# Residuals and squares made piece by piece at the borders, modulation tiles set into attention waits, eight gate units set into the second attention

## The chip, the cores and the metric

One core of one Trainium2 chip runs the whole program. The metric is the device time of one execution in microseconds (us), median of several runs.

## What is computed

Two transformer blocks over 256 tokens of width 2048, all in f32. The parts that matter here, cut from the reference:

```python
def first_block(...):
    for layer in range(2):
        mod = silu(c) @ ada_w[layer] + ada_b[layer]
        shift, scale, gate = split(mod)
        h = rmsnorm(x, norm_g[layer]) * (1 + scale) + shift
        ...                     # layer 0: attention of 8 heads and convolution; layer 1: spatial gating
        x = x + gate * (mixed @ w_out)
    return rmsnorm(x, final_g)

def second_block(x, c, ...):
    sh1, sc1, g1, sh2, sc2, g2 = split(silu(c) @ w_ada + b_ada)
    h = rms_norm(x, norm1_w) * (1 + sc1) + sh1
    q, k, v, f_logit, u, gate_s, gate_a = split(h @ w_in)
    y_ssm = half_glu(s5_mixer(u, ...), w_glu, b_glu)
    y_attn = fox_attention(q, k, v, f_logit, ...)          # 8 heads, causal, forget gates
    merged = sigmoid(gate_s) * (y_ssm @ w_ssm_up) + sigmoid(gate_a) * (y_attn @ w_attn_up)
    x = x + g1 * (merged @ w_out)
    h2 = rms_norm(x, norm2_w) * (1 + sc2) + sh2
    return x + g2 * peer_ffn(h2, ...)                      # 128 experts per token, gathered by row
```

## The kernel before

Everything lies with features in partitions: x, h and proj hold tiles of 128 features by 256 tokens (TOK), 16 tiles for a width of 2048 (DT). A matrix product is a row of **units**. A unit is one output tile: 16 matmuls of 128x128 weights by 128x256 into a bank of PSUM (G0 or G1, in turn), done by `dense` and `unit` (L417). ScalarE takes each unit out of its bank (`leave`, L860), with the gate's factor where it feeds a residual (`leave_gated`). Weights come in chunks of 1 MB, one per unit, through a ring of four slots: SyncE issues a load as soon as the units of the chunk four back are done. The order of the stages is the list STREAM (L60), and the host packs the weights in that order; each engine's program is written out by hand in the same order, and engines meet at semaphores.

The stages in order: `first`, `ev`, `kv`, `ez`, `zb` (projections of layer 0, with the first attention among them), `ev_out`, `od`, `od_out` (layer 1), `w_in`, `glu`, `ssm_up`, the second attention, `attn_up`, `gates` (32 units), `w_out`, `peer_q`, then the experts.

**Modulation tiles.** Each output of `silu(c) @ ada_w` is a dot product of a row of 2048 on VectorE (`ada_tile`, L1238), a tile of 1 MB at a time, 16 tiles to a group. Tiles come through a second ring of four (`aring`), whose loads GpSimd issues when VectorE has used the tile four back (L382). Group g must be done before its shift, scale or gate is used. `ada_part(g, first, count)` places tiles in VectorE's program.

**Borders.** Between two blocks x gets its residual, the squares of x are summed over features, and the root of the mean scales x. `add_residual` (L1543) waits for each four tiles of h, adds them to x (L1548), squares them (L1539) and adds the four squares up (L1215); TensorE sums over partitions with a matrix of ones into B7 (`feature_sum_of_fours`, L468); ScalarE takes the root (`std`, L882), VectorE the reciprocal (L1223) and writes x/rms into h by fours (L1556); ScalarE applies scale and shift (`modulate`, L892), after which the next dense stage can start on tile 0. At `ev_out` VectorE's program has modulation groups 1 and 2 whole ahead of `add_residual`, at `od_out` group 6. After `od_out` there are two normalizations in a row: the last of the first block, with weight final_g, made in x (L1604), and the first of the second block, on squares of its result.

**Attention.** Per head: TensorE makes scores, VectorE maxima, ScalarE exponentials, VectorE probabilities, TensorE turns them (L531), ScalarE copies them (L920), TensorE multiplies with the values (L538), VectorE takes the result (`finish`). `softmax`, `softmax_steps` and `attention` take a table `between` of what each engine does after head hh. In the first attention that is a `zb` unit on TensorE and two or three modulation tiles on VectorE; in the second, after heads 0, 2, 4 and 6, one chunk of `ssm_up`, which is four output tiles of 4 matmuls each.

**Gates.** After `attn_up` 32 gate units follow: 16 of gate_s into proj 0 to 15 and 16 of gate_a. VectorE multiplies them with the up results and adds the halves; `merged` lets `w_out` start. Modulation groups 7 and 8 stand ahead of this, group 9 between the first 16 products and the rest.

## Time and profile before

| | us |
|---|---|
| median of 3 runs | 3271.11 (3262.88 to 3278.96) |
| profiled execution, its own time | 3271.55 |
| its span, first to last instruction | 3269.7 |
| TensorE busy (matmul) | 2762.1, 84% |
| VectorE busy | 2081.1, 64% |
| GpSimd busy | 840.3, 26% |
| ScalarE busy | 579.1, 18% |
| mean granted clock of TensorE | 0.899 of full |

Busy time on TensorE is a poor measure of what it achieves, since its clock has two levels, 1.2 and 2.4 GHz (0.5 and 1.0 of full in the views). What bounds the end is read from the chain of waits; where TensorE stops or runs slowly is read from the timeline and from the granted clock of short windows.

### The profile page before, as it was taken

How to read it: one execution, taken by the hardware profiler on the slowest of the kernel's cores; microseconds unless marked ns; L12 is line 12 of the kernel's file. 1: busy time of each engine (PE TensorE's matmuls, PEld its weight loads, DVE VectorE, ACT ScalarE, POOL GpSimd, SP SyncE). 2: the span in 40 equal slices, each digit the busy share in tenths (PEclk: the TensorE clock that was granted, in tenths of full speed). 3: DMA queues.
4: the chain of work that ended last, by engine and by line, in shares of the span. 5: the costliest groups of instructions: out<-in, count | busy, mean ns of one | idle time of the engine just before them, and what ended most of it. 6: DMA issues, size and time to landing. Idle time of an engine off the chain costs nothing.

```text
span 3269.7 us, 31515 instructions
## 1 busy us (share of the span) xinstructions
PE 2762.1 (84%) x12106; PEld 2206.7 (67%) x12106; DVE 2081.1 (64%) x2892; ACT 579.1 (18%) x1102; POOL 840.3 (26%) x724
## 2 busy tenths in 40 slices
...
GB/s 375 383 390 134 112 195 396 301 188 355 305 355 280 157 107 113 122 44 140 421 262 268 143 140 408 374 382 418 421 421 387 380 337 206 385 399 390 378 397 267
DMA packets 158373, 951.27 MB, mean 291 GB/s; under 512 B 17584, under 2 KB 17584, under 8 KB 69808
## 3 DMA queue, kind: packets, MB, share of 16 engines
...
## 4 chain that ended last, share of the span: by engine, by line
PE 41%; DVE 23%; DMA 23%; ACT 6%; issue 4%; POOL 2%; DVEq 0%; ACTq 0%; POOLq 0%
PE G L417 33%; DMA acc<-v_rows,proj 12%; DMA aring<-ada 7%; DVE vec L1830 3%; DVE aring L1238 3%; DVE aring L1802 2%; ACT vec L1116 2%; PE M L810 2%; DVE ring L1802 2%; DVE proj L1319 2%; DVE proj L1489 1%; DMA aring<-peer_u,proj 1%; PE G L798 1%; DMA ring<-peer_u,proj 1%; DVE proj L1843 1%
## 5 line engine op out<-in xcount | busy, mean ns | idle before, releaser
L417 PE MATMUL G<-h,ring 128*128 128x256 f32 x4928 | 1084.6, 383 | 13.2 <-ACT h L892 13.2
L417 PEld LDWEIGHTS G<-h,ring 128*128 128x128 f32 x4928 | 944.8, 192 | 147.4 <-issue 16.5
L382 POOL DMA_DIRECT2D aring<-ada x208 | 109.8, 529 | 1631.3 <-DVE mods L1238 1624.3
L1238 DVE CUSTOM_DVE_ANT_0 aring<-aring,acc,vec 128x2048 f32<-128x2048 f32 x176 | 410.9, 2350 | 174.8 <-DMA aring<-ada 173.5
L417 PE MATMUL G<-proj,ring 128*128 128x256 f32 x2080 | 462.0, 386 | 10.6 <-DVE proj L1595 4.8
L1830 DVE SCALAR_TENSOR_TENSOR vec<-acc,dots,vec 128x1024 f32<-128x1024 f32 x254 | 325.9, 1283 | 203.7 <-DMA acc<-v_rows,proj 201.4
L417 PEld LDWEIGHTS G<-proj,ring 128*128 128x128 f32 x2080 | 402.9, 194 | 69.9 <-issue 12.8
L849 PE MATMUL M<-sq,mix 128*128 128x512 f32 x1024 | 442.5, 595 | 1.8 <-ACT mix L1130 1.1
L849 PEld LDWEIGHTS M<-sq,mix 128*128 128x128 f32 x1024 | 195.3, 191 | 248.4 <-issue 245.5
L405 POOL DMA_INDIRECT acc<-v_rows,proj x256 | 274.1, 1071 | 316.1 <-DVE vec L1830 293.3
L397 POOL DMA_INDIRECT aring<-peer_u,proj x128 | 219.7, 1716 | 347.3 <-DVE proj L1768 222.8
L1802 DVE CUSTOM_DVE_ANT_0 aring<-sq,aring 128x2048 f32<-128x2048 f32 x108 | 245.4, 2290 | 29.5 <-DMA aring<-peer_u,proj 19.1
L860 ACT ACTIVATE proj<-G 128x256 f32 (+1 forms) x170 | 65.3, 384 | 980.6 <-PE G L417 980.4
L397 POOL DMA_INDIRECT ring<-peer_u,proj x112 | 209.1, 1867 | 102.1 <-PE M L810 31.3
L1802 DVE CUSTOM_DVE_ANT_0 ring<-sq,ring 128x2048 f32<-128x2048 f32 x91 | 207.1, 2290 | 17.4 <-DMA ring<-peer_u,proj 16.3
L820 PE MATMUL B<-h,acc 128*128 128x128 f32 x704 | 97.4, 305 | 51.9 <-ACT acc L1140 29.0
L1140 ACT ACTIVATE acc<-M 128x1024 f32<-128x1024 f32 x86 | 86.9, 1024 | 269.1 <-PE M L810 268.9
L798 PE MATMUL G<-vec 128*128 128x128 f32 x256 | 59.1, 405 | 88.1 <-ACT vec L1124 85.7
L820 PEld LDWEIGHTS B<-h,acc 128*128 128x128 f32 x704 | 95.3, 221 | 54.8 <-issue 30.4
L798 PEld LDWEIGHTS G<-vec 128*128 128x128 f32 x256 | 49.9, 290 | 95.2 <-ACT vec L1124 92.7
L810 PE MATMUL M<-cst,ring 128*128 128x128 f32 x336 | 63.2, 368 | 56.8 <-DMA ring<-peer_u,proj 56.8
L1548 DVE TENSOR_TENSOR x<-x,h 128x1024 f32<-128x1024 f32 x12 | 14.7, 1225 | 151.3 <-ACT h L860 151.2
...
## 6 DMA issues: line engine op xcount, KB each, us to landing
...
sq<-v_blocks SPq DMA_DIRECT2D x128, 512.0 KB
...
acc<-v_rows,proj POOLq DMA_INDIRECT x256, 6.8
...
```

Source lines behind the costliest of these rows:

```text
L382: pool.dma_start(aring[:, n % SLOTS, :], ada[a]).then_inc(ada_in[n % SLOTS], 16)
L397: pool.indirect_dma_start(u_slot(n), None, peer_u, where).then_inc(u_in[ROW_SLOT[n]], 16)
L405: pool.indirect_dma_start(v_ring[:, n % VSLOTS, :], None, v_rows, where).then_inc(v_in[n % VSLOTS], 16)
L417: mm = nc.tensor.matmul(bank[:, 0:TOK], lhsT=ring[:, slot, weights_at + t * P:weights_at + (t + 1) * P], rhs=rhs[:, t, :], start=(t == 0), ...
L798: mm = nc.tensor.matmul(G[n % 2][:, k * P:(k + 1) * P], lhsT=far[:, k * P:(k + 1) * P], rhs=near[:, k * P:(k + 1) * P], start=True, stop=True)
L810: mm = nc.tensor.transpose(M[:, j * P:(j + 1) * P], u_slot(n)[:, j * P:(j + 1) * P], ident)
L820: mm = nc.tensor.matmul(O[k % 2][:, 0:P], lhsT=turned_row[:, j * P:(j + 1) * P], rhs=tokens, start=(j == 0), stop=(j == DT - 1))
L849: mm = nc.tensor.matmul(M[:, tk * HALF + half * 512:tk * HALF + (half + 1) * 512], lhsT=mix[tk][:, j, :], rhs=blocks[:, j % BSLOTS, half * ...
L1140: nc.scalar.activation(turned_row[:, half * 1024:(half + 1) * 1024], M[:, half * 1024:(half + 1) * 1024], ACT.Copy).then_inc(row_kept, 1)
L1238: V_.tensor_tensor_reduce(out=tile, in0=tile, in1=vector, scale=1.0, scalar=bias, op0=ALU.mult, op1=ALU.add, accum_out=column).then_inc(ad ...
L1802: V_.tensor_tensor_reduce(out=u_slot(n), in0=sq[:, tk * D:(tk + 1) * D], in1=u_slot(n), scale=1.0, scalar=0.0, op0=ALU.mult, op1=ALU.add, ...
L1830: V_.scalar_tensor_tensor(out=y, in0=v_ring[:, n % VSLOTS, :], scalar=c, in1=y, op0=ALU.mult, op1=ALU.add).then_inc(v_added, 1)
```

## The change

1. `PIECES` cuts the 16 tiles into 4, 4, 4, 3 and 1. `add_residual(name, k)` does one piece, and the pieces stand among the modulation tiles of `ev_out` and `od_out`; at `w_out` they follow each other. The pieces of 3 and 1 are not added up on VectorE; TensorE sums each of their tiles. x/rms goes into h as 1, 3, 4, 4, 4.
2. Between the two blocks only one pass of squares is left. gs2 is final_g squared; TensorE sums squares as they are (B7) and weighted with gs2 (B6), piece by piece among the units of `od_out`. var2 is the product of the weighted sum and 1/rms squared, h is x times the product of both reciprocals, and final_g goes into the scale gs. The values of x itself are normalized after the second attention.
3. The tiles of group 0 and five of group 1 are spread over the waits ahead of and in the first attention (a new table `waiting`, ahead of the wait for the values product).
4. Eight units of gate_a (tiles 4 to 7 and 12 to 15) leave the gates stage: fill0 ahead of glu, fill1 (three) ahead of the second attention, fill2 to fill5 after heads 1, 3, 5 and 7. `gates` has 24 units. ScalarE makes their sigmoid in two operations at `attn_up`.
5. Group 9 of the modulation tiles is cut in two halves, before and behind unit 20 of the gates.

```diff
+PIECES = ((0, 4), (4, 4), (8, 4), (12, 3), (15, 1))
...
-          ("glu", 1, 4), ("ssm_up", 4, 4), ("attn_up", 8, 2), ("gates", 32, 1), ("w_out", 16, 1), ("peer_q", 16, 1)]
+          ("fill0", 1, 1),
+          ("glu", 1, 4), ("fill1", 3, 1), ("up0", 1, 4), ("fill2", 1, 1), ("up1", 1, 4), ("fill3", 1, 1), ("up2", 1, 4),
+          ("fill4", 1, 1), ("up3", 1, 4), ("fill5", 1, 1), ("attn_up", 8, 2), ("gates", 24, 1), ("w_out", 16, 1), ("peer_q", 16, 1)]
...
+            def sum_piece(t, n, added):
+
+                sums[0] += 1
+                pe.wait_ge(sum_in, sums[0])
+                if n == 4:
+                    at = t * TOK if added is sq else t * P
+                    return nc.tensor.matmul(B7[:, 0:TOK], lhsT=ones, rhs=added[:, at:at + TOK], start=(t == 0), stop=False)
+                for e in range(t, t + n):
+                    mm = nc.tensor.matmul(B7[:, 0:TOK], lhsT=ones, rhs=sq[:, e * TOK:(e + 1) * TOK], start=False,
+                                          stop=(e == DT - 1))
+                return mm
+
+            def residual_sum():
+
+                for t, n in PIECES:
+                    mm = sum_piece(t, n, sq)
                 mm.then_inc(sum_done, 1)
+
+            def residual_sums(k):
+
+                t, n = PIECES[k]
+                mm = sum_piece(t, n, att)
+                if k == len(PIECES) - 1:
+                    mm.then_inc(sum_done, 1)
+                for e in range(t, t + n):
+                    mm = nc.tensor.matmul(B6[:, 0:TOK], lhsT=gs2[:, e:e + 1].to_broadcast([P, P]), rhs=sq[:, e * TOK:(e + 1) * TOK],
+                                          start=(e == 0), stop=(e == DT - 1))
+                if k == len(PIECES) - 1:
+                    mm.then_inc(both_sums, 1)
 
...
-            dense("od_out", [proj])
-
-
-            feature_sum_of_fours()
-            feature_sum(sq, DT, 4)
+            dense("od_out", [proj], first=0, count=6)
+            residual_sums(0)
+            dense("od_out", [proj], first=6, count=4)
+            residual_sums(1)
+            dense("od_out", [proj], first=10, count=4)
+            residual_sums(2)
+            dense("od_out", [proj], first=14, count=2)
+            residual_sums(3)
+            residual_sums(4)
...
+            dense("fill0", [h])
...
             pe.wait_ge(ssm_g, 4)
             dense("glu", [proj, proj, proj, proj], k=4)
+            dense("fill1", [h], count=1)
             pe.wait_ge(head_used, 1)
             head_rows_spread(8, row=1)
...
+            dense("fill1", [h], first=1, count=1)
...
+            dense("fill1", [h], first=2, count=1)
...
-                      {0: lambda: ssm_up(0), 2: lambda: ssm_up(1), 4: lambda: ssm_up(2), 6: lambda: ssm_up(3)})
+                      {0: lambda: ssm_up(0), 1: lambda: dense("fill2", [h]), 2: lambda: ssm_up(1), 3: lambda: dense("fill3", [h]),
+                       4: lambda: ssm_up(2), 5: lambda: dense("fill4", [h]), 6: lambda: ssm_up(3), 7: lambda: dense("fill5", [h])})
             pe.wait_ge(o_read, 16)
             dense("attn_up", [proj[:, 12:20, :], proj[:, 12:20, :]], k=8)
-            dense("gates", [h], count=16)
-            dense("gates", [h], first=16, count=16)
+            dense("gates", [h])
...
+                    if hh in waiting:
+                        waiting[hh]()
                     dve.wait_ge(pv_done, base + hh + 1)
...
             head_inverse(1)
+            ada_part(0, 0, 1)
             step(head_scale(sq[:, 0:1024], 4, V("k_norm")), on=rot_in)
+            ada_part(0, 1, 3)
             step(rope(kv_keys[:, :, 0:TOK], 2, 2), on=qk_ready)
+            ada_part(0, 4, 3)
...
-                    {0: lambda: ada_part(0, 0, 3), 1: lambda: ada_part(0, 3, 2), 2: conv_centre,
-                     3: lambda: ada_part(0, 5, 3), 4: lambda: ada_part(0, 8, 2), 5: conv_scale,
-                     6: lambda: ada_part(0, 10, 3), 7: lambda: ada_part(0, 13, 3)})
+                    {0: lambda: ada_part(0, 8, 1), 1: lambda: ada_part(0, 10, 1), 2: conv_centre,
+                     3: lambda: ada_part(0, 13, 1), 4: lambda: ada_part(0, 15, 1), 5: conv_scale,
+                     6: lambda: ada_part(1, 2, 1), 7: lambda: ada_part(1, 4, 1)},
+                    {0: lambda: ada_part(0, 7, 1), 1: lambda: ada_part(0, 9, 1), 2: lambda: ada_part(0, 11, 1),
+                     3: lambda: ada_part(0, 12, 1), 4: lambda: ada_part(0, 14, 1), 5: lambda: ada_part(1, 0, 1),
+                     6: lambda: ada_part(1, 1, 1), 7: lambda: ada_part(1, 3, 1)})
...
+            def add_residual(name, k, added=None):
+
+                t, n = PIECES[k]
+                dve.wait_ge(unit_evac, UNIT0[name] + t + n)
+                xs, squares = flat(x[:, t:t + n, :]), sq[:, t * TOK:(t + n) * TOK]
+                step(tt(xs, xs, flat(h[:, t:t + n, :]), ALU.add))
+                step(tt(squares, xs, xs, ALU.mult), on=None if n == 4 else sum_in)
+                if n == 4:
+                    add_tiles(squares if added is None else added[:, 512 * k:512 * k + 512], squares, 4)
+
+            def scaled_into_h(by):
+
+                for t, n in ((0, 1), (1, 3), (4, 4), (8, 4), (12, 4)):
+                    step(tt(h[:, t:t + n, :], x[:, t:t + n, :], over_tiles(by, n), ALU.mult), on=h_scaled)
 
...
+            ada_part(1, 5, 7)
+            add_residual("ev_out", 0)
+            ada_part(1, 12, 4)
+            ada_part(2, 0, 3)
+            add_residual("ev_out", 1)
+            ada_part(2, 3, 7)
+            add_residual("ev_out", 2)
+            ada_part(2, 10, 6)
+            add_residual("ev_out", 3)
+            add_residual("ev_out", 4)
...
-            ada_group(6)
-            add_residual("od_out")
+            step(tt(gs2[:, :], V("final_g"), V("final_g"), ALU.mult))
+            norm_weight(gs[:, :], V("norm1_w"), mod("scale2"))
+            step(tt(gs[:, :], gs[:, :], V("final_g"), ALU.mult))
+            for k in range(len(PIECES)):
+                if k < 4:
+                    ada_part(6, 4 * k, 4)
+                add_residual("od_out", k, added=att)
             root()
-            for t in range(DT):
-                V_.scalar_tensor_tensor(out=x[:, t, :], in0=x[:, t, :], scalar=V("final_g")[:, t:t + 1], in1=rstd[:, :],
-                                        op0=ALU.mult, op1=ALU.mult).then_inc(x_normed, 1)
-                if t % 4 == 3:
-                    dve.wait_ge(x_normed, t + 1)
-                    square_four(t // 4, add_up=False)
-            normed_into_h(V("norm1_w"), mod("scale2"))
-            mods_from(6)
+            dve.wait_ge(both_sums, 1)
+            step(tt(var2, rstd[:, :], rstd[:, :], ALU.mult))
+            step(tt(var2, var2, B6[:, 0:TOK], ALU.mult), on=var_in)
+            sums["std"] += 1
+            dve.wait_ge(std_ready, sums["std"])
+            step(V_.reciprocal(var2, var2))
+            step(tt(var2, var2, rstd[:, :], ALU.mult))
+            scaled_into_h(var2)
...
+            act.wait_ge(unit_evac, UNIT0["attn_up"])
+            for t in (20, 44):
+                nc.scalar.activation(flat(proj[:, t:t + 4, :]), flat(proj[:, t:t + 4, :]), ACT.Sigmoid).then_inc(filled, 1)
...
+            for t in range(DT):
+                V_.scalar_tensor_tensor(out=x[:, t, :], in0=x[:, t, :], scalar=V("final_g")[:, t:t + 1], in1=rstd[:, :],
+                                        op0=ALU.mult, op1=ALU.mult).then_inc(x_normed, 1)
...
             step(tt(part(8, 8), part(8, 8), part(28, 8), ALU.mult))
-            ada_group(9)
-            dve.wait_ge(unit_evac, gates + 28)
-            step(tt(part(16, 8), part(16, 8), sq[:, 2048:4096], ALU.mult))
+            dve.wait_ge(filled, 2)
+            step(tt(part(20, 4), part(20, 4), sq[:, 3072:4096], ALU.mult))
+            step(tt(part(44, 4), part(44, 4), part(40, 4), ALU.mult))
+            step(tt(part(4, 4), part(4, 4), part(20, 4), ALU.add))
+            step(tt(part(12, 4), part(12, 4), part(44, 4), ALU.add))
+            ada_part(9, 0, 8)
+            dve.wait_ge(unit_evac, gates + 20)
+            step(tt(part(16, 4), part(16, 4), sq[:, 2048:3072], ALU.mult))
+            step(tt(part(0, 4), part(0, 4), part(16, 4), ALU.add))
+            ada_part(9, 8, 8)
+            dve.wait_ge(unit_evac, gates + 24)
             step(tt(part(24, 4), part(24, 4), part(36, 4), ALU.mult))
-            step(tt(part(0, 12), part(0, 12), part(16, 12), ALU.add))
-            dve.wait_ge(unit_evac, gates + 32)
-            step(tt(part(44, 4), part(44, 4), part(40, 4), ALU.mult))
-            step(tt(part(12, 4), part(12, 4), part(44, 4), ALU.add), on=merged)
+            step(tt(part(8, 4), part(8, 4), part(24, 4), ALU.add), on=merged)
```

TensorE at the end of `od_out`, in the changed kernel (G are the units' banks, L423 the dense helper, L475 and L477 the plain sums, L494 the weighted ones):

```order
L423 MATMUL G<-proj,ring 128x256 x96
L475 MATMUL B<-att,cst 128x256
L494 MATMUL B<-sq,gs 128x256 x4
L423 MATMUL G<-proj,ring 128x256 x64
L475 MATMUL B<-att,cst 128x256
L494 MATMUL B<-sq,gs 128x256 x4
L423 MATMUL G<-proj,ring 128x256 x32
L477 MATMUL B<-sq,cst 128x256 x3
L494 MATMUL B<-sq,gs 128x256 x3
L477 MATMUL B<-sq,cst 128x256
L494 MATMUL B<-sq,gs 128x256
L423 MATMUL G<-h,ring 128x256 x64
```

Before, 4 and then 16 plain sums stood between the last unit of `od_out` and the first of `w_in`; now three groups of five stand among the units, and eight matmuls behind them.

TensorE from the head sums to the first scores of the second attention, before (L489 spreads the inverse norms, L710 turns the values, L513 is a head's scores):

```order
L479 MATMUL B<-sq,cst 8x256 x8
L489 MATMUL M<-dots,cst 128x256 x8
L417 MATMUL G<-proj,ring 128x256 x16
L489 MATMUL M<-dots,cst 128x256 x8
L710 MATMUL M<-cst,proj 128x128 x16
L513 MATMUL M<-proj 128x256
```

And now (L516, L744 and L540 are the same steps):

```order
L506 MATMUL B<-sq,cst 8x256 x8
L423 MATMUL G<-h,ring 128x256 x16
L516 MATMUL M<-dots,cst 128x256 x8
L423 MATMUL G<-proj,ring 128x256 x16
L423 MATMUL G<-h,ring 128x256 x16
L516 MATMUL M<-dots,cst 128x256 x8
L423 MATMUL G<-h,ring 128x256 x16
L744 MATMUL M<-cst,proj 128x128 x16
L423 MATMUL G<-h,ring 128x256 x16
L540 MATMUL M<-proj 128x256
```

Four gate units (those that read h) stand among the steps.

VectorE at unit 20 of the gates, in the changed kernel (L1283 is a modulation tile, its second row reads the accumulator):

```order
L1283 ISA aring,mods<-aring,acc,vec 128x2048
L1283 ISA mods 128x1
L1779 TENSOR_TENSOR proj<-proj,sq 128x1024
L1780 TENSOR_TENSOR proj<-proj 128x1024
L1283 ISA aring,mods<-aring,acc,vec 128x2048
L1283 ISA mods 128x1
```

Eight tiles stand ahead of L1779 and eight behind L1780; behind those come the last product and sum (L1783, L1784). Before, all sixteen stood between the products of unit 16 and those of unit 28.

## Rows read from the trace of the kernel before

**Rows 1.** The page, chain that ended last: shares of the span by line.

```profile
PE G L417 33%; DMA acc<-v_rows,proj 12%; DMA aring<-ada 7%; DVE vec L1830 3%; DVE aring L1238 3%; DVE aring L1802 2%; ACT vec L1116 2%; PE M L810 2%; DVE ring L1802 2%; DVE proj L1319 2%; DVE proj L1489 1%; DMA aring<-peer_u,proj 1%; PE G L798 1%; DMA ring<-peer_u,proj 1%; DVE proj L1843 1%
```

**Rows 2.** Timeline of TensorE: start, duration, line, tiles, count, idle before and releaser.

```profile
504.35 110.77 PE L417 MATMUL G<-proj,ring 128*128 128x256 f32 x512 [1.59 <-DVE proj L1533]
...
641.55 127.30 PE L417 MATMUL G<-h,ring 128*128 128x256 f32 x576 [4.40 <-ACT h L892]
...
1147.29 30.33 PE L417 MATMUL G<-h,ring 128*128 128x256 f32 x128 [4.41 <-ACT h L892]
```

**Rows 3.** Timeline of all engines, the border from ev_out to od.

```profile
615.15 0.47 ACT L860 ACTIVATE h<-G,mods 128x256 f32<-128x256 f32 x1 [6.43 <-PE G L417]
...
621.09 1.22 DVE L1548 TENSOR_TENSOR x<-x,h 128x1024 f32<-128x1024 f32 x1
...
635.93 1.22 PE L468 MATMUL B<-sq,cst 128*128 128x256 f32 x2 [2.49 <-DVE sq L1215]
...
637.76 1.75 DVE L1223 RECIPROCAL rstd<-rstd 128x256 f32<-128x256 f32 x1 [1.68 <-ACT rstd L882]
...
640.80 7.97 ACT L892 ACTIVATE h<-h,mods,gs 128x256 f32<-128x256 f32 x16 [3.15 <-DVE h L1556]
```

**Rows 4.** Timeline of VectorE and of TensorE, first attention.

```profile
399.07 0.42 DVE L1511 TENSOR_TENSOR proj<-B,proj 128x256 f32<-128x256 f32 x1 [2.56 <-PE B L538]
...
418.19 1.09 PE L531 MATMUL M<-cst,att 128*128 128x128 f32 x8 [1.21 <-DVE att L1303]
```

**Rows 5.** Timeline of ScalarE, last eviction of od_out.

```profile
1121.08 0.47 ACT L860 ACTIVATE h<-G,mods 128x256 f32<-128x256 f32 x1 [6.43 <-PE G L417]
```

**Rows 6.** Timeline of TensorE, glu to attn_up.

```profile
1404.04 8.86 PE L417 MATMUL G<-proj,ring 128*128 128x256 f32 x32
...
1412.83 5.00 PE L489 MATMUL M<-dots,cst 8*128 8x256 f32 x16
...
1420.33 3.68 PE L710 MATMUL M<-cst,proj 128*128 128x128 f32 x16 [2.51 <-DVE proj L1272]
...
1435.25 1.22 PE L513 MATMUL M<-proj 128*128 128x256 f32 x2 [2.90 <-ACT att L912]
...
1445.22 9.06 PE L417 MATMUL G<-proj,ring 128*128 128x256 f32 x32
...
1457.39 0.66 PE L531 MATMUL M<-cst,att 128*128 128x128 f32 x4
...
1458.73 1.13 PE L538 MATMUL B<-sq,proj 128*128 128x256 f32 x4 [0.69 <-ACT sq L920]
...
1469.30 8.97 PE L417 MATMUL G<-proj,ring 128*128 128x256 f32 x32
...
1529.37 55.52 PE L417 MATMUL G<-proj,ring 128*128 128x256 f32 x256 [0.88 <-DVE proj L1692]
```

**Rows 7.** Windows of TensorE: length, busy (count), granted clock, DMA share, GB/s.

```profile
1466.00:1469.00 3.00, 2.31 (x8) 0.50 0.00 0
1475.00:1478.00 3.00, 3.00 (x16) 1.00 0.00 0
```

**Rows 8.** End of the gates: timelines, group 9's tiles, window of all engines.

```profile
1695.93 2.29 DVE L1704 TENSOR_TENSOR proj<-proj,sq 128x2048 f32<-128x2048 f32 x1 [51.18 <-ACT proj L860]
...
L1238 DVE CUSTOM_DVE_ANT_0 aring<-aring,acc,vec x16: 2346/2351/2352, 1700.6 to 1753.6; 128x2048 f32<-128x2048 f32 x16
...
1720.00:1750.00 30.00, 30.00 (x140) 26.41 (x140) 17.27 (x15) 1.54 (x4) 2.63 (x5) 1.00 1.02 423
...
1807.68 1.22 DVE L1713 TENSOR_TENSOR proj<-proj 128x1024 f32<-128x1024 f32 x1
...
1809.23 110.77 PE L417 MATMUL G<-proj,ring 128*128 128x256 f32 x512 [3.33 <-DVE proj L1713]
```

**Rows 9.** Timeline of TensorE, end of w_out and start of peer_q.

```profile
1919.84 3.73 PE L738 MATMUL M<-cst,mods 128*128 128x128 f32 x32
...
1929.70 15.74 PE L417 MATMUL G<-h,ring 128*128 128x256 f32 x64 [4.40 <-ACT h L892]
```

72 lines of the change are left out of this document (32 added, 40 removed).

## The prediction, made before the change was run

> **What bounds the kernel now.** The chain that ended last comes first [rows 1]: its largest share, 33% of the span, is TensorE in the dense helper (L417), so what delays the next dense stage delays the end. The timeline of TensorE then shows where it stops between stages [rows 2]: `ev_out` ran 504.35 to 615.1, and `od` began only at 641.55. A dense unit (16 matmuls of 128x256) takes 110.77/16 = 6.9 us, one matmul 0.43. The timeline of all engines over that border [rows 3] shows what fills it: VectorE, busy with modulation tiles, makes its first residual at 621.09, when `ev_out` is long over. In the second attention the timeline of TensorE [rows 6] and its granted clock [rows 7] show waits inside the heads and stretches at 1.2 GHz: glu's 16 matmuls took 8.86 us there, and four up units 9.06, where 6.9 is the full price.
>
> **First attention.** Five more modulation tiles leave the stage behind it, and one tile per head goes into VectorE's wait for the values product. That wait is 2.56 us at head 0 and a tile takes 2.35 [rows 4, 8], so it is hidden; if a tile has not landed, its delay shows. Seven tiles ahead of the heads lie in rotation and norm waits and cost nothing. TensorE's own work stays; what it gains is its waits for the probabilities, 1.21 us at head 2 [rows 4] and a like one at head 5: 1.2 x 2 = **-2.4 us** (ends 0 and -4).
>
> **First border, `ev_out` to `od`.** Now four tiles of x are added and squared as they come; only tile 15 is left at the end. From the end of the last unit, E: TensorE adds 7 sums instead of 4, 7 x 0.43 = 3.0, the last of which needs tile 15's square. That square is ready at E + 0.5 (eviction, as the ACTIVATE of [rows 3]) + 2 x 0.46 (a 128x256 operation is 0.42 [rows 4]) + 0.1 = 1.5, so the sums decide: E + 3.2 with the drain of the last. Then sum end to reciprocal 0.6 (635.93 + 1.22 to 637.76), reciprocal 1.8, first tile of h 0.45 instead of a group of 1.22, bias and scale to matmul 0.75 (640.80 to 641.55): E + 6.8 [rows 2, 3]. I add 0.5, since tiles 1 to 3 come as one group. The gap was 641.55 - 615.1 = 26.4, so **-19.1 us**. It needs the tiles of groups 1 and 2 done before unit 15. In seven tiles four lie in the ring, and the others come every (1753.6 - 1700.6 - 4 x 2.3) / 11 = 4.0 us, the step of tiles that wait for the transfer [rows 8]. With a residual group after units 4, 8 and 12 (27.7 us apart), seven tiles take 4 x 2.3 + 3 x 4.0 = 21 us and fit; the last six start 3.7 us after unit 12 and take 17.2, which ends them as unit 15 arrives and 7 us before unit 16. If they are late, the last pieces are what is late next, at most some 5 us. Ends -14 and -21.
>
> **Second border, `od_out` to `w_in`.** One normalization, its square pass and its second root go: the second variance is the sum of squares weighted by final_g squared, times 1/rms squared. From the last eviction T = 1121.08 to `w_in` at 1147.29 it was 26.2 us [rows 2, 5]. Now: TensorE has 6 matmuls for piece 3 and then 1 for piece 4, T + 3.2 with drain; root and reciprocal 0.6 + 1.8; two 128x256 products on VectorE 0.9; root again 0.7; reciprocal 1.8; product 0.45; first tile 0.45; bias to matmul 0.75: T + 10.7, and 0.5 for the group: 11.2, a gain of 15.0. But the weighted sums cost TensorE 5 matmuls for each of the three first pieces in the middle of the stage, on the path: 15 x 0.43 = 6.5. **-8.5 us** (ends -5 and -10). The 16 normalizing operations move behind the second attention, 16 x 0.42 = 6.7 us of VectorE, covered by its 51.18 us wait at 1695.93 [rows 8].
>
> **Second attention.** Eight gate units, 8 x 6.9 = 55.3 us, leave the gates stage and stand in this one. The new stretch from 1404.04, at full clock: fill0 6.9; glu 6.9; a fill 6.9; spread 3.5 (5.00 was at half clock); a fill 6.9, which covers VectorE's 2.35 before the turning; turning 1.9 (3.68 at half); a fill 6.9, which covers ScalarE's copy; scores 3.2 (from the end of the four up units, 1454.2, to 1457.39); wait for the exponentials 2.9; scores 3.2; turn, copy, product 2.5 (1457.39 to 1458.73 + 1.13) [rows 6]. Sum 51.7. A pair of heads is then 2 x (6.9 + 3.2 + 2.5) = 25.2 instead of 1469.30 - 1445.22 = 24.1: in it the fill costs 1.1. Three pairs 75.6; up, turn and product of the last head 9.4; fill5 6.9. Total 143.6, and 4 us that I allow for stretches at 1.2 GHz around the opening wait, the size of the loss seen on glu and the first up units: 147.6, where it was 1529.37 - 1404.04 = 125.3. So +22.3 - 55.3 = **-33.0 us**. The price of the clock is the least known of all: [rows 7] has 0.50 in the low part of a pair and 1.00 at the end of its up units. If every one of the eight fills and four ups began slow (9.06 - 6.91 = 2.2 each) 22 us would come on top of no allowance, 18 against mine; with no slow stretch it is 4 better. Ends -15 and -37. I take the value near full clock because after the change the low part of a head is followed by 6.9 us of dense work, where before two such parts stood together.
> The Trainium skill (TensorE: Matmul & The Clock Gate, Part 1: The HAM clock gate) says that the slow clock is the default and activity releases it. By that alone the stretch would run at full clock, and the allowance of 4 us would go. The trace agrees in kind: 1.00 at 1475, 0.50 at 1466.
>
> **End of the gates.** Here something is taken back. Sixteen tiles of group 9 used to follow unit 16, and ran 1700.6 to 1753.6 + 2.35 = 1755.9: 55.3 us, since they come at the pace of the transfers (1720 to 1750: DMA share 1.02, 423 GB/s) [rows 8]. Then 50 us were left. Now 8 units, not 16, follow. From T0, where VectorE starts on unit 16's product (1695.93): products 4.7, four 128x1024 operations for the gates made early 5.0, so tiles start at T0 + 9.7; 55.3 of tiles, with the 2.5 us for unit 20 between them covered by the transfer; T0 + 65.0; then a product and a sum, 2.5: `merged` at T0 + 67.5, TensorE at + 67.8. The gates end at T0 - 0.5 + 8 x 6.9 = T0 + 54.8. TensorE stands 13.0 us instead of 3.33, and starts at 1.2 GHz, about 1.2 us more (half of the 2 us that the up units lost, for there is no low work ahead): **+10.9 us**. Queued behind the second eight tiles are unit 24's product, and behind that `w_out`. Ends +5 and +15.
> The Trainium skill (DMA: Bandwidth & Descriptors, Issuing engines are not separate DMA queues) says that loads issued from different engines run on the same 16 DMA engines and interleave. By it the wait stays, since modulation tiles and weights share them; if they did not share, sixteen tiles would take 16 x 2.3 = 37 us and the term would be zero.
>
> **Third border, `w_out` to `peer_q`.** TensorE first makes g3 (3.6 us from 1919.84), then 7 sums 3.0, drain and root 0.8, reciprocal 1.8, tile 0.45, 0.75: 10.4, where it was 1929.70 - 1919.84 = 9.9 [rows 9]. **+0.5 us** (0 to 1). What was late there was VectorE; now it is TensorE's sums.
>
> **Sum.** -2.4 - 19.1 - 8.5 - 33.0 + 10.9 + 0.5 = -51.6. The profiled execution took 3271.55 us, which gives 3219.9; the median of the runs is 0.4 lower, so I say **3220 us**. Everything behind `w_out` (the experts) is only shifted.
>
> **Rivals.**
> *The clock falls once in each pair.* The fills do not keep it up: one up unit group at 9.06 (+2.1) and one low part as in [rows 6] at double price (+2.8) per pair, 4 x 4.9 - 4 = +15.6: 3236. For it: the 0.50 that stands in every pair now. Against it: low parts that follow dense work end at 1.00. Chance 0.17.
> *The modulation tiles come in time at the gates.* Then `merged` waits for unit 24 only and the +10.9 goes: 3209. For it: 3.33 us was the whole wait. Against: the transfer share of 1.02. Chance 0.10.
> *Slower: the second attention runs at 1.2 GHz throughout.* TensorE has some 130 us of work in the new stretch; all of it at half clock is +130 less my 4: 3346. It decides from 52 us on, when more than 40% of that work is slow. For it: from the second spread to the first up units the matmuls of [rows 6] went at half pace (3.68 for the turning). Against: the waits that kept it low are the ones filled. Chance 0.02.
> The forecast has 0.65; 0.06 is left to a border whose gain fails in part (the first at its end -14, the second at -5: 3228) or wholly (3247).
>
> **Range and chances.** The range takes in both nearer rivals and their spread with the bounds of the border terms: 3209 less 5 for the better end of the second attention, 3236 plus 7 for the borders' ends: 3204 to 3243. The likeliest case alone is 3210 to 3230. About 0.5% (16 us) can be told from no change: faster 0.94, within it 0.04, slower 0.02.
>
> **What would show it.** The gap before `od` near 7 us and before `w_in` near 11 from the last eviction; 15 matmuls into B6 and B7 inside `od_out`; pairs of 25 us with clock at or above 0.9; about 13 us of wait before `w_out`, ended by VectorE, with the last tiles ended by DMA. Wrong would be: pairs near 30 us; a residual that starts late after unit 16; a `w_out` that starts within 4 us.

## The result, and the profile after

The changed kernel takes **3231.07 us** (median of 4 runs, 3224.2 to 3235.47), the kernel before on the same chip 3273.87 (4 runs): a ratio of 0.9872, 95% interval 0.984 to 0.9904. That is 42.8 us or 1.3% faster. Forecast were 3220 us and a range of 3204 to 3243: right in direction and inside the range, 11 us short of the gain.

Timeline of TensorE in the changed kernel, in the order of the stages. The columns are those of [rows 2]; the dense helper is L423 now. The profile has two records for each matmul of the program: the 16 matmuls of a unit stand as x32, so a pair of records (x2) is one matmul, and the counts below are records.

```profile
503.35 110.77 PE L423 MATMUL G<-proj,ring 128*128 128x256 f32 x512 [1.55 <-DVE proj L1586]
613.96 1.46 PE L475 MATMUL B<-sq,cst 128*128 128x256 f32 x6
615.25 1.89 PE L477 MATMUL B<-sq,cst 128*128 128x256 f32 x8
620.75 0.67 PE L423 MATMUL G<-h,ring 128*128 128x256 f32 x2 [3.60 <-ACT h L927]
...
986.58 43.39 PE L423 MATMUL G<-proj,ring 128*128 128x256 f32 x192 [4.56 <-DVE proj L1653]
...
1115.91 30.12 PE L423 MATMUL G<-h,ring 128*128 128x256 f32 x128 [6.94 <-ACT h L927]
...
1530.86 55.42 PE L423 MATMUL G<-proj,ring 128*128 128x256 f32 x256
...
1764.73 112.83 PE L423 MATMUL G<-proj,ring 128*128 128x256 f32 x512 [12.70 <-DVE proj L1784]
1877.40 3.73 PE L773 MATMUL M<-cst,mods 128*128 128x128 f32 x32
...
1887.76 0.67 PE L423 MATMUL G<-h,ring 128*128 128x256 f32 x2 [3.60 <-ACT h L927]
```

The starts of the stages make a ledger. "Before" is the same difference in the kernel before [rows 2, 6, 8, 9]; the predicted column regroups the terms of the sum.

| stretch of TensorE | before | after | difference | predicted |
|---|---|---|---|---|
| up to `ev_out` | 504.35 | 503.35 | -1.0 | -2.4 |
| `ev_out` to `od` | 137.20 | 117.40 | -19.8 | -19.1 |
| `od` to `od_out` | 367.03 | 365.83 | -1.2 | 0 |
| `od_out` to `w_in` | 138.71 | 129.33 | -9.4 | -8.5 |
| `w_in` to `attn_up` | 382.08 | 414.95 | **+32.9** | **+22.3** |
| `attn_up` to `w_out` | 279.86 | 233.87 | -46.0 | -45.6 |
| `w_out` to `peer_q` | 120.47 | 123.03 | +2.6 | +1.7 |
| start of `peer_q` | 1929.70 | 1887.76 | -41.9 | -51.6 |

The -41.9 up to `peer_q` is close to the 42.8 us between the medians. The two profiled executions differ by 47.3 us; the other 5.4 lie behind `peer_q`, where no work was changed, and are within the scatter of that stretch (below). All the terms but one came within 1.5 us; the second attention cost 10.6 us more than predicted. Its timeline on TensorE: the head sums and fill0, a spread of head rows and glu, the opening, and some rows of the pairs of heads (the shape is weights, then what is streamed; `8*128 8x256` contracts over 8 rows, `128*8 128x256` over 128 rows into 8 columns):

```profile
1365.28 3.62 PE L506 MATMUL B<-sq,cst 128*8 128x256 f32 x16
1368.83 7.17 PE L423 MATMUL G<-h,ring 128*128 128x256 f32 x32
1375.93 3.71 PE L516 MATMUL M<-dots,cst 8*128 8x256 f32 x16
1379.58 8.86 PE L423 MATMUL G<-proj,ring 128*128 128x256 f32 x32
...
1414.59 0.59 PE L540 MATMUL M<-proj 128*128 128x256 f32 x2
1415.11 0.70 PE L544 MATMUL M<-cst,att 8*128 8x256 f32 x2
...
1420.83 1.22 PE L540 MATMUL M<-proj 128*128 128x256 f32 x2 [2.90 <-ACT att L947]
...
1430.80 8.87 PE L423 MATMUL G<-proj,ring 128*128 128x256 f32 x32
1439.50 0.59 PE L540 MATMUL M<-proj 128*128 128x256 f32 x2
...
1442.77 0.66 PE L558 MATMUL M<-cst,att 128*128 128x128 f32 x4
...
1457.57 7.07 PE L423 MATMUL G<-proj,ring 128*128 128x256 f32 x32
...
1469.09 2.07 PE L565 MATMUL B<-sq,proj 128*128 128x256 f32 x4 [0.69 <-ACT sq L955]
1470.95 7.58 PE L423 MATMUL G<-h,ring 128*128 128x256 f32 x32
...
1482.98 2.08 PE L565 MATMUL B<-sq,proj 128*128 128x256 f32 x4 [0.69 <-ACT sq L955]
1484.85 9.14 PE L423 MATMUL G<-proj,ring 128*128 128x256 f32 x32
```

A group of 32 matmuls takes 7.07 us at full clock; here glu took 8.86, and three behind it 8.87, 7.58 and 9.14. The product with the values (L565) takes 1.13 at full clock and 2.07 and 2.08 in the two rows here. Windows of TensorE in the changed kernel (length, busy and count, granted clock, DMA share, GB/s) show the two levels beside each other. The last window is the whole stretch, from the end of the head sums to `attn_up`:

```profile
1424.00:1427.00 3.00, 3.00 (x7) 0.50 0.00 0
1447.00:1450.00 3.00, 3.00 (x15) 1.00 0.00 0
1484.00:1487.00 3.00, 3.00 (x9) 0.50 0.00 0
...
1368.83:1530.86 162.03, 153.63 (x626) 0.89 0.23 78
```

That stretch was 128.98 us in the kernel before, at 0.74, and is 162.03 now, at 0.89. The clock did rise, but not to full.

### The profile page after: what moved, and what is told of

Same layout as the page of the kernel before. It is cut to its first block, busy times and chain, and to the rows that moved or that the text cites. A ratio compares the mean times of both kernels' runs of the same rounds, so it can differ in the third digit from the quotient of the medians.

```text
span 3222.4 us, 31476 instructions
## 1 busy us (share of the span) xinstructions
PE 2747.6 (85%) x12124; PEld 2203.6 (68%) x12124; DVE 2076.1 (64%) x2899; ACT 577.1 (18%) x1101; POOL 841.1 (26%) x724
## 4 chain that ended last, share of the span: by engine, by line
PE 47%; DVE 21%; DMA 19%; ACT 6%; issue 4%; POOL 2%; DVEq 0%; ACTq 0%; POOLq 0%
PE G L423 37%; DMA acc<-v_rows,proj 12%; DMA aring<-ada 5%; DVE vec L1903 3%; DVE aring L1283 2%; ACT vec L1161 2%; PE M L845 2%; DVE ring L1875 2%; DVE proj L1366 2%; DVE aring L1875 1%; DVE proj L1536 1%; PE G L833 1%; DVE proj L1916 1%; ACT vec L1166 1%; DMA ring<-peer_u,proj 1%
## 5 line engine op out<-in xcount | busy, mean ns | idle before, releaser
L423 PE MATMUL G<-h,ring 128*128 128x256 f32 x4928 | 1086.1, 382 | 14.6 <-ACT h L927 14.6
L423 PEld LDWEIGHTS G<-h,ring 128*128 128x128 f32 x4928 | 944.1, 192 | 149.9 <-issue 17.9
L1283 DVE CUSTOM_DVE_ANT_0 aring<-aring,acc,vec 128x2048 f32<-128x2048 f32 x176 | 410.1, 2350 | 133.4 <-DMA aring<-ada 131.3
L423 PE MATMUL G<-proj,ring 128*128 128x256 f32 x2080 | 462.4, 385 | 18.8 <-DVE proj L1784 12.7
L423 PEld LDWEIGHTS G<-proj,ring 128*128 128x128 f32 x2080 | 402.9, 194 | 77.6 <-issue 15.8
L895 ACT ACTIVATE proj<-G 128x256 f32<-128x256 f32 (+1 forms) x170 | 65.2, 383 | 1013.7 <-PE G L423 1013.6
L1594 DVE TENSOR_TENSOR x<-x,h 128x1024 f32<-128x1024 f32 (+2 forms) x15 | 15.2, 1012 | 191.9 <-ACT h L895 191.9
```

Of the source, the lines that this page charges most:

```text
L423: mm = nc.tensor.matmul(bank[:, 0:TOK], lhsT=ring[:, slot, weights_at + t * P:weights_at + (t + 1) * P], rhs=rhs[:, t, :], start=(t == 0), ...
L1283: V_.tensor_tensor_reduce(out=tile, in0=tile, in1=vector, scale=1.0, scalar=bias, op0=ALU.mult, op1=ALU.add, accum_out=column).then_inc(ad ...
```

## The experiments

Each is the changed kernel with one edit, unless its text says otherwise. Ratios are to the kernel before on the same chip; the changed kernel's own is 0.9872. The median of the kernel before was 3268.42 to 3273.87 us on these chips, so medians of different rows compare less well than ratios do. The table holds the stretches of the profiled runs on which the verdicts rest. "Attention" is the one from the end of the head sums to `attn_up`.

| kernel | `ev_out` to `od` | `od_out` to `w_in` | attention, clock | `attn_up` to `w_out` | median us | ratio, 95% interval |
|---|---|---|---|---|---|---|
| before | 137.20 | 138.71 | 128.98, 0.74 | 279.86 | 3273.87 | 1 |
| changed | 117.40 | 129.33 | 162.03, 0.89 | 233.87 | 3231.07 | 0.9872 (0.984 to 0.9904) |
| tiles early | 117.39 | 129.33 | 165.40 | 224.44 | 3217.71 | 0.9828 (0.9801 to 0.9854) |
| no fills | 117.39 | 129.33 | 128.38, 0.73 | 279.86 | 3239.91 | 0.9901 (0.9875 to 0.9927) |
| fill in the wait | 117.40 | 129.33 | 160.27, 0.90 | 233.93 | 3230.17 | 0.9871 (0.9843 to 0.99) |
| full rows | 117.39 | 129.33 | 144.64, 0.98 | 234.02 | 3210.3 | 0.9805 (0.9779 to 0.9831) |
| two passes | 117.39 | 135.66 | 164.12 | 233.58 | 3232.4 | 0.9899 (0.987 to 0.9928) |
| residual behind | 117.40 | 130.22 | 162.15 | 234.01 | 3226.89 | 0.9871 (0.9851 to 0.9891) |
| five tiles back | 126.09 | 129.76 | 165.41 | 233.87 | 3245.39 | 0.9922 (0.9891 to 0.9953) |
| full rows, kernel before | 137.07 | 139.18 | 106.43, 0.87 | 279.86 | 3251.85 | 0.9942 (0.9923 to 0.9961) |
| full rows and early tiles | 117.39 | 129.32 | 144.64, 0.98 | 224.44 | 3198.58 | 0.9789 (0.9765 to 0.9813) |
| the same, and full spreads | 117.40 | 129.33 | 141.93, 0.99 | 224.44 | 3195.38 | 0.9769 (0.9747 to 0.9791) |

Three scatters bound what a single profiled run can say. Eight runs whose program is the same up to `ev_out` started it between 499.97 and 506.68 us. The same second attention took 162.03 to 165.41 us in five runs. And from `peer_q` to the end, the same work in all twelve kernels of the table, it was 1330.5 to 1344.4 us. A stretch is therefore compared with its like, and neither -1.0 us up to `ev_out` nor the 5.4 behind `peer_q` can be told from nothing.

### The tiles of group 9, ahead of the gates

```diff
             ada_group(8)
+            ada_part(9, 0, 10)
...
-            ada_part(9, 0, 8)
+            ada_part(9, 10, 3)
...
-            ada_part(9, 8, 8)
+            ada_part(9, 13, 3)
```

> Sixteen modulation tiles of group 9 stand 10 behind group 8, ahead of VectorE's wait for the gates, then 3 and 3 between the gates' products (in the changed kernel 8 and 8 between the products). Theory (the late end of the merged sum is the tiles' transfer pace): ten tiles fall into VectorE's 47.6 us of idle time before the gates, the last product ends with the gates, and w_out's wait falls from 12.70 us to about 3.3; w_out itself falls from 112.8 to about 110.8 us, since TensorE no longer stands still long enough to come back at a low clock. Together -11.4 us, about 3220 us, a ratio to the kernel before of 0.984. Rival (what holds the sum is the products' and ScalarE's order, not the tiles): the wait stays over 10 us and the time at 3231 us. A second rival (the tiles are held by the transfers wherever they stand): the ten tiles end only at about 1740 us, the wait falls to some 8 us, -5 us.

First the changed kernel, timeline of VectorE: the first tile of group 9, the eighth, the last, and the sum that lets `w_out` start.

```profile
1707.02 2.35 DVE L1283 CUSTOM_DVE_ANT_0 aring<-aring,acc,vec 128x2048 f32<-128x2048 f32 x1
...
1727.20 2.35 DVE L1283 CUSTOM_DVE_ANT_0 aring<-aring,acc,vec 128x2048 f32<-128x2048 f32 x1 [1.99 <-DMA aring<-ada]
...
1759.61 2.35 DVE L1283 CUSTOM_DVE_ANT_0 aring<-aring,acc,vec 128x2048 f32<-128x2048 f32 x1 [1.98 <-DMA aring<-ada]
...
1763.15 1.23 DVE L1784 TENSOR_TENSOR proj<-proj 128x1024 f32<-128x1024 f32 x1
```

Then the run with early tiles, where the lines are one further on: the last product (L1784), which now waits for ScalarE, the sum behind it (L1785), and `w_out`.

```profile
1754.93 1.23 DVE L1784 TENSOR_TENSOR proj<-proj 128x1024 f32<-128x1024 f32 x1 [18.20 <-ACT proj L895]
1756.19 1.22 DVE L1785 TENSOR_TENSOR proj<-proj 128x1024 f32<-128x1024 f32 x1
```

```profile
1757.74 112.43 PE L423 MATMUL G<-proj,ring 128*128 128x256 f32 x512 [3.26 <-DVE proj L1785]
```

The wait before `w_out` fell from 12.70 to 3.26 us, 9.4 us as expected: the late end of the gates was the pace of the tiles where they stood. VectorE, whose program was full there, now stands 18.20 us for the gates. The second part of the expectation fell: `w_out` takes 112.43 us, not 110.8. Its clock starts low after a wait of 3.26 us as it does after 12.70. Whether it does after 3.3 us differs from run to run: in the kernel before `w_out` to `peer_q` took 120.47 us [rows 8, 9], and 122.16 with the same code and wait in the run of that kernel with full rows. Both rivals fell: the wait is under 4 us, and the ten tiles had ended by 1690.0 us, 9.8 us before VectorE's first product of the gates.

### Without the fills

```diff
-            dense("fill0", [h])
...
-          ("fill4", 1, 1), ("up3", 1, 4), ("fill5", 1, 1), ("attn_up", 8, 2), ("gates", 24, 1), ("w_out", 16, 1), ("peer_q", 16, 1)]
+          ("glu", 1, 4), ("up0", 1, 4), ("up1", 1, 4), ("up2", 1, 4),
+          ("up3", 1, 4), ("attn_up", 8, 2), ("gates", 32, 1), ("w_out", 16, 1), ("peer_q", 16, 1)]
```

> The eight gate units are back among the gates (32 of them, group 9 whole ahead of the last products, as in the kernel before); the borders and the first attention stay as changed. Theory of the sum: the fills cost the second attention +33.1 us and the end of the gates +11.4 us and save 55.3 us of gates, a net of -10.8 us; so this kernel takes +10.8 us, about 3242 us, a ratio to the kernel before of 0.990, and its stretch from the end of the head sums to attn_up is again about 129 us, its wait before w_out about 3.3 us. If the fills are worth what was predicted for them (-22), it would be 3253 us and the stretch shorter than 129 us. If they are worth nothing, 3231 us.

Measured: 3239.91 us, the stretch back at 128.38 us, `attn_up` to `w_out` back at 279.86. So the fills, with what they do to the end of the gates, are worth 8.8 us in the medians. The stretches say 10.2: +33.7 in the attention, -46.0 up to `w_out`, +2.1 up to `peer_q`. That agrees within the scatter with the 10.8 expected, and the two first borders are the same to 0.01 us, so they don't lean on the fills.

### A fill inside the opening wait

```diff
                 scores(0)
+                opening()
                 for hh in range(HEADS):
...
-            dense("fill1", [h], first=2, count=1)
...
+                      opening=lambda: dense("fill1", [h], first=2, count=1))
```

> The third unit of fill1, which ran ahead of the second attention, stands between the scores of its first and its second head, where TensorE waited some 2 to 3 us with nothing to do. Theory A (standing still there is what brings the clock down at 1423 to 1432 us): that dip goes, scores of head 1 take 3.2 us instead of 6.3 and the first PV 2.5 instead of 3.7, and the wait of 2 us or so is filled: about -6 us in the stretch up to attn_up (162.1 to about 156), dips later in the attention stay or shift. Theory B (the dips come from the attention's own matmuls, whatever stands between): a dip stays within 10 us of the opening and the stretch gets shorter by the filled wait alone, -1 to -2 us. Total 3225 us under A, 3230 under B.

TensorE in this run, from the first scores on:

```profile
1408.74 0.70 PE L540 MATMUL M<-proj 128*128 128x256 f32 x2 [1.97 <-ACT proj L1089]
1409.37 1.16 PE L544 MATMUL M<-cst,att 8*128 8x256 f32 x2
...
1414.47 9.75 PE L423 MATMUL G<-h,ring 128*128 128x256 f32 x32
1424.05 0.59 PE L540 MATMUL M<-proj 128*128 128x256 f32 x2
```

The wait of 2.90 us is gone, but the unit no longer covers ScalarE's copy of the values, so 1.97 us stand ahead of the first scores. The clock was low from then on, and the fill itself took 9.75 us. Three more low stretches follow in the pairs (from 1441, 1482 and 1495 us), where TensorE had waited 0.69 us at most. The stretch is 160.27 us and the total the same, as theory B had it; 1.8 us less is within the scatter of this stretch, though. For the opening the run decides nothing: the low clock there stands behind a wait again, the new one of 1.97 us. The low stretches in the pairs, behind 0.69 us, are what speaks for B.

### All rows in the scores' extra matmuls

```diff
-nc.tensor.matmul(o, lhsT=cum[:, qt * P:(qt + 1) * P], rhs=pick_rows(hh),
+nc.tensor.matmul(o, lhsT=att[:, 1024 + qt * P:1024 + (qt + 1) * P], rhs=pick_rows(hh),
...
-mm = nc.tensor.matmul(o, lhsT=pick_rows(hh)[:, 0:P], rhs=ncum, start=False, stop=True)
+mm = nc.tensor.matmul(o, lhsT=pick_rows(hh)[:, 0:P], rhs=att[:, 1280:1536], start=False, stop=True)
...
-                return ident[0:8, hh:hh + 1].to_broadcast([8, TOK])
+                return ident[:, hh:hh + 1].to_broadcast([P, TOK])
```

> The extra matmuls that the scores of the second attention carry, which contract over 8 rows in the changed kernel, contract over all 128 rows, with operands that give the same sums; nothing else changes. Theory C (matmuls that use few rows let the clock fall): the dips to 0.50 and 0.59 at 1423 to 1516 us go, and the stretch from the head sums to attn_up takes 152 us instead of 162, about 3221 us in all. Theory A (only standing still counts): the dips stay where they are, 162 us, no difference beyond 3 us. If more columns or rows make a matmul longer, the stretch would be longer at the same clock: +2 us or more.

This is the run that settles it. Timeline of TensorE, one pair of heads, and the window of the whole stretch:

```profile
1453.62 7.07 PE L423 MATMUL G<-proj,ring 128*128 128x256 f32 x32
1460.52 0.59 PE L540 MATMUL M<-proj 128*128 128x256 f32 x2
1460.95 0.60 PE L544 MATMUL M<-cst,att 128*128 128x256 f32 x2
...
1463.12 0.60 PE L558 MATMUL M<-cst,att 128*128 128x128 f32 x4
1464.40 1.13 PE L565 MATMUL B<-sq,proj 128*128 128x256 f32 x4 [0.69 <-ACT sq L955]
...
1477.12 7.07 PE L423 MATMUL G<-proj,ring 128*128 128x256 f32 x32
```

```profile
1372.06:1516.70 144.64, 136.25 (x626) 0.98 0.26 88
```

The identity's column that picks the head is zero in every row but the head's own, so what stands in the added rows of the other operand does not count; here these are old finite values, not zeros. The same number of matmuls, the same waits of 0.69 and 2.90 us, and every pair takes 23.5 us, with all its fills and up units at 7.07. The scores of head 1, behind the wait of 2.90, are still slow (4.4 us instead of 2.6), and so is glu. The stretch falls by 17.4 us, where theory C had expected 10. Of these 5.4 are plain speed: the six pairs of score matmuls of a head take 2.60 us (1460.52 to 1463.12) instead of 3.27 (1439.50 to 1442.77), since those of 8 rows start 0.54 us apart per pair and those of 128 rows 0.43; 0.67 x 8. The other 12.0 are clock. In the medians it is 20.8 us.

### The same edit on the kernel before

```diff
-                return ident[0:8, hh:hh + 1].to_broadcast([8, TOK])
+                return ident[:, hh:hh + 1].to_broadcast([P, TOK])
```

with the two operands `att` in `attention` as above.

> The kernel before, with one edit: the extra matmuls of the second attention's scores contract over 128 rows instead of 8, as in the run with full rows of the changed kernel. Theory C (matmuls over few rows let the clock fall): the dips in heads 3, 5 and 7 go, 5.0 us each, and the two extra pairs of matmuls run at 0.43 instead of 0.54 to 0.63 us from start to start, 0.69 us a head: the stretch from the head sums to attn_up falls from 129.0 to about 109 us, total about 3252 us, ratio 0.994. The fills would then cost the stretch 144.6 - 109 = 35.6 us. Theory A (the waits of 1.11 and 0.69 us in every second head bring it down): the dips stay, the stretch falls by the 0.69 us a head alone, to about 124 us, and the fills also help the clock by closing the waits. Half of the opening at the low clock may stay in either case, since the matmuls that spread the head rows, over 8 rows too, are left as they are.

The stretch took 106.43 us, at 0.87, and the median is 3251.85 us, where 3252 had been expected. So the kernel before lost even more to this, 22.6 us of which 5.4 are plain speed and some 17 clock. Within the heads two dips stayed, and both stand right behind a wait (glu, the second spread, the turning and the first scores stayed low in part as well, as had been left open):

```profile
1440.97 1.22 PE L513 MATMUL M<-proj 128*128 128x256 f32 x2 [2.90 <-ACT att L912]
...
1497.85 0.96 PE L513 MATMUL M<-proj 128*128 128x256 f32 x2 [1.11 <-ACT att L912]
1498.60 1.06 PE L517 MATMUL M<-cst,att 128*128 128x256 f32 x2
```

This gives the price of the fills with full rows: 144.64 - 106.43 = 38.2 us, where they cost 33.1 with the low rows. The fills help the clock in both. Adding up, over this stretch, by how much each group of matmuls is longer than the same group at full clock gives about 28 us for the kernel before and 15 for the changed one, 11 and 3.6 with full rows (a count from the timelines, good to a microsecond or so). So the fills gave back some 13 us of clock with the low rows and 7 with full rows; 5.2 is the difference of the two.

### The second border with its two passes

```diff
-            dense("od_out", [proj], first=0, count=6)
-            residual_sums(0)
...
-            scaled_into_h(var2)
+            dense("od_out", [proj])
+            residual_sum()
+            feature_sum(sq, DT, 4)
...
+            normed_into_h(V("norm1_w"), mod("scale2"))
```

> The second border goes back to the two passes of squares of the kernel before (residuals, x times final_g, squares, and the sums in two passes behind od_out); the pieces of the sums inside od_out and the 16 final products elsewhere go with it; all else stays as changed. Theory (the border was shortened by 9.4 us by this part alone): the time from the last od_out eviction to w_in goes from 10.35 us back to about 26 us less what the sums in od_out cost (6.5 us), so the kernel takes about +9 us, 3240 us, ratio 0.990. Rival (the modulation tiles in the border's neighbourhood, not the squares, set its length): the border stays within 3 us of 10.35 and od_out gets 6.5 us shorter, -6 us.

The border from the last eviction (1097.63) to `w_in` (1120.50) took 22.9 us instead of 10.35, and the stage without sums was 6.2 us shorter: +6.3 us in the stretch. The rival fell; the part is worth 6.3 of the 9.4 us, and I had expected the 9. The other 3.1 go to what this run keeps, the small pieces at the end of the sums and at the start of h; the order of the tiles can't be it, since VectorE stood 23.95 us for the last evictions here in the kernel before. No run takes the small pieces away by themselves. The median moved by 1.3 us only and the ratio by 0.0027; neither can tell 6 us from the scatter of these runs, the stretch can.

### The residual behind the tiles

```diff
-            ada_part(1, 5, 7)
+            ada_part(1, 5, 11)
+            ada_group(2)
...
-            ada_part(1, 12, 4)
-            ada_part(2, 0, 3)
...
-            ada_part(2, 3, 7)
...
-            ada_part(2, 10, 6)
```

> In the first border the pieces of the residual all stand behind the 27 modulation tiles of the ev_out stage; in the changed kernel they stand among them. Theory (VectorE has 27 tiles at 4.0 us each to make in this stage and is done with them before ev_out's last pieces leave, so the order among them is worth nothing): od still starts 6 to 8 us after the last eviction of ev_out, 0 us of difference, 3231 us. Rival (having the pieces interleaved is what shortened the border): the residual pieces pile up behind the last tile and od starts 5 us or more later, 3237 us or more.

117.40 us, as in the changed kernel to the hundredth. The tiles ended at 599.7, the piece of three at 612.7, the last unit's eviction at 614.0. Here the interleaving is worth nothing, because the tiles end 14 us before the last unit: the three groups of four, 3.7 us each on VectorE, still fit in. Where the tiles end late it is another matter, as the next run shows.

### Five tiles back

```diff
-            ada_part(0, 0, 1)
...
-            ada_part(0, 1, 3)
...
-            ada_part(0, 4, 3)
...
+                    {0: lambda: ada_part(0, 0, 3), 1: lambda: ada_part(0, 3, 2), 2: conv_centre,
+                     3: lambda: ada_part(0, 5, 3), 4: lambda: ada_part(0, 8, 2), 5: conv_scale,
+                     6: lambda: ada_part(0, 10, 3), 7: lambda: ada_part(0, 13, 3)})
...
-            ada_part(1, 5, 7)
+            ada_part(1, 0, 8)
```

> The first two groups of modulation tiles stand again where the kernel before has them, so that 32 tiles instead of 27 fall into the ev_out stage (and none ahead of the first attention, and the attention's are in clumps again); the pieces of residual, squares and sums stay as changed. Theory (the transfers bring a tile every 4.0 us or so, and the tiles, not the squares, set when VectorE gets to the last pieces): the last tile ends five tiles, some 20 us, later than 607 us less the slack it has now, od starts some 10 us later, at about 630 us, total +9 us, 3240 us. Rival (the squares made by pieces were the whole gain of this border): od starts at 620.75 us still, and the first attention is 1.0 us longer: 3232 us.

The rest of groups 1 and 2 follows in eights between the pieces. VectorE and TensorE at the border:

```profile
622.82 2.35 DVE L1283 CUSTOM_DVE_ANT_0 aring<-aring,acc,vec 128x2048 f32<-128x2048 f32 x1 [1.06 <-DMA aring<-ada]
625.09 0.95 DVE L1588 TENSOR_TENSOR x<-x,h 128x768 f32<-128x768 f32 x1
```

```profile
627.09 3.42 PE L477 MATMUL B<-sq,cst 128*128 128x256 f32 x8 [7.00 <-DVE sq L1589]
634.12 6.33 PE L423 MATMUL G<-h,ring 128*128 128x256 f32 x14 [3.60 <-ACT h L927]
```

The tiles come every 3.8 us (603.86 to 622.82 in five steps) and the last ends at 625.1, when `ev_out`'s last eviction, at 618.8, is over. `od` starts 8.7 us later in its stretch: 126.09 instead of 117.40. So of the 19.8 us of this border the five tiles are worth 8.7. The other 11.1 are what the pieces give when the tiles are late: after the last tile only the pieces of 3 and 1 are left, 2.9 us of VectorE, where the kernel before had four groups of 3.7 us there. Three of those four, 11.1 us, now stand among the tiles. That is the interleaving, by this account from the timelines; with the tiles early it isn't needed. No run has late tiles with the small pieces behind them.

The median is 14 us up. Of the 22.3 us between the two profiled runs 8.7 are this border, 4.7 lie ahead of `ev_out`, 3.4 in the second attention and 4.1 behind `peer_q`, the last two no more than the scatters allow. Ahead of `ev_out` the edit also brings the waits of 1.21 us at heads 2 and 5 of the first attention back, and its start at 508.03 is 1.4 us later than the latest of the eight.

### Both finds together, and full rows in the spreads

First the edits of full rows and of early tiles in one kernel:

```diff
+            ada_part(9, 0, 10)
...
-                return ident[0:8, hh:hh + 1].to_broadcast([8, TOK])
+                return ident[:, hh:hh + 1].to_broadcast([P, TOK])
```

> Both finds together: the extra matmuls of the second attention's scores over 128 rows, and ten tiles of group 9 ahead of the gates. They lie in different stretches, and each by itself gave: the stretch from the head sums to attn_up 144.6 us instead of 162.0 (-17.4), the wait before w_out 3.3 instead of 12.7 and w_out 2 us shorter (-11.4). If they add, the kernel takes 3231 - 28.8 = about 3202 us, ratio to the kernel before 0.979. Rival (the gates now start 17 us earlier, so the tiles of group 9, which come at the transfers' pace, are late again): the wait before w_out is back at 6 us or more, 3206 us or more.

3198.58 us, ratio 0.9789, against 0.979 expected. The stretches are 144.64 and 224.44 us: the gains add, and the tiles are in time though the gates start earlier. The stretch of 144.64 us is made up otherwise than in the run with full rows, though: the unit behind the second spread is slow, and the scores of head 1 are not (0.43 us from one pair to the next).

```profile
1398.67 8.86 PE L423 MATMUL G<-h,ring 128*128 128x256 f32 x32
...
1421.68 0.70 PE L540 MATMUL M<-proj 128*128 128x256 f32 x2 [2.90 <-ACT att L947]
```

Then that kernel with one more edit:

```diff
+            step(V_.memset(dots[:, :, :, :], 0.0))
...
-                                          lhsT=ident[0:HEADS, j:j + 1].to_broadcast([HEADS, P]),
-                                          rhs=head_rows[:, row, :], start=True, stop=True)
+                                          lhsT=ident[:, j:j + 1].to_broadcast([P, P]),
+                                          rhs=dots[:, row, :, :].rearrange("p b c -> p (b c)"), start=True, stop=True)
```

> The kernel with full rows and early tiles, and the matmuls that spread head rows to 128 partitions (over 8 rows, ahead of both attentions) now over 128 rows as well, with zeros in the rows that don't count, written once at the start. Theory C (matmuls over few rows let the clock fall): the low clock behind them goes: the spread at 326 us takes 3.7 instead of 5.0 us and the units behind it are 2.1 us shorter, those behind the spread at 367 us 1.8 us shorter, glu 7.07 instead of 8.86 us: -7 us against the run with full rows and early tiles. Rival (a spread's 16 matmuls are too short a stretch, and it is the changes from one operand shape to another or the waits around them that bring the clock down): glu stays at 8.86 us and the time is the same within 2 us.

```profile
1375.29 3.62 PE L516 MATMUL M<-dots,cst 128*128 128x256 f32 x16
1378.74 7.07 PE L423 MATMUL G<-proj,ring 128*128 128x256 f32 x32
...
1417.23 1.22 PE L540 MATMUL M<-proj 128*128 128x256 f32 x2 [2.90 <-ACT att L947]
```

glu takes 7.07 us, for the first time in any of these kernels; it was 8.86 to 8.87 in all the others. The unit behind the second spread takes 7.07 too. So the matmuls over 8 rows were the cause there as well; and since a spread's 16 all have one shape, no change of shape among them is needed for it. But the stretch fell by 2.7 us and the total by 3.2, not 7, and the intervals of the two ratios overlap. The spread at 326 us had been at full clock already in the run with full rows and early tiles, so there was nothing to gain there, and the one at 367 us stands behind a wait of 4.79 us and is still slow. The opening wait of 2.90 us caught the clock this time. It has the lowest median of the kernels run: 3195.38 us.

## Why the prediction was right, and what it missed

**First attention, -2.4.** TensorE's waits at heads 2 and 5 are gone as predicted. With the tiles put back they are there again, 1.21 us each, so the tiles made them. At head 7 nothing was won: 1.74 us for VectorE and 2.47 for ScalarE became 4.43 for ScalarE. The -1.0 measured is smaller than the scatter of this point, so the size of the gain is open.

**First border, -19.1: right** (-19.8), and by its own steps: a gap of 6.8 us from unit end to `od` was worked out, and 614.0 to 620.75 is 6.8. The half microsecond added for the group of three was not needed. The run with five tiles back shows the condition that it stated, the tiles done before unit 15. That "four tiles of x are added and squared as they come" mattered less than the text has it: with the residual wholly behind the tiles the border was the same 117.40 us.

**Second border, -8.5: right** (-9.4). From the last eviction at 1105.56 to `w_in` it is 10.35 us; 10.7 was worked out, and 0.5 added in vain again. The sums inside the stage cost what was charged.

**Second attention, +22.3 of a net -33.0: the filled waits right, the clock wrong.** The step that failed is the allowance: "4 us that I allow for stretches at 1.2 GHz". From glu's place in the kernel before, the new stretch is 162.03 - 3.65 = 158.4 us, where 143.6 had been counted at full clock: the low clock took 14.8 us, not 4 (the count by groups above gives 15). The reason I gave for a value near full clock, that each low part is now followed by dense work, was only partly true. By the count above the stretch lost some 28 us to the clock before; 24 of them were to go, and 13 did. The rest of the cause was in the low part itself, which full rows showed (12.0 of the 15 us went), and I had read past it: the spread in [rows 6] has `8*128 8x256` as its shape, two of the three pairs of matmuls of every score have it too, and I priced them by time alone. The rival of one fall in each pair gave 3236; the kernel ended between it and the forecast, 5 us from the one and 11 from the other, with a low stretch at the opening and three more behind it (from 1469, 1483 and 1510 us). As a mechanism that rival, at 0.17, was the nearer one. The text also adds up its worst case wrongly: eight fills and four up units at 2.2 us each are 26 us, not 22, which would have moved the end of -15 to -11. It changes neither the forecast nor the range.
The Trainium skill (TensorE: Matmul & The Clock Gate, Part 1: The HAM clock gate) has the gate follow how busy the engine has been. Several of the low stretches stand behind waits, as it would have it (0.50 behind the 2.90 us at the opening). But 16 matmuls over 8 rows, back to back for 3.71 us, were followed by glu at 8.86 us, and the same 16 over 128 rows by glu at 7.07: there the measurement goes further than the page. Few columns do not do the same: the head sums, over 128 rows into 8 columns, were followed by fill0 at 7.17 us.

**End of the gates, +10.9: right.** The wait is 12.70 us where 13.0 was worked out, +9.4 in the ledger. The clock's part was 2.1 us instead of 1.2 (112.83 - 110.77), and the run with early tiles shows that it doesn't go with the length of the wait. The rival with the tiles in time was wrong for the kernel as it is, but it pointed at the edit that takes 9.4 us out of this stretch and 13 from the median.

**Third border, +0.5: right**: 1877.40 to 1887.76 is 10.4 us.

**What stays open.** Which of the low stretches a given run has is not settled: after the same 2.90 us of waiting the clock was 0.50 in one run and full in another of the same code there (full rows and early tiles: scores of head 1 at 0.59 a pair). The 1.2 us less between `od` and `od_out` can't be told from scatter: it took 365.4 to 367.9 us in the runs that share the changed kernel's code there, and 369.6 in the kernel before with full rows. How many rows would be enough is not known, since only 8 and 128 were run.
